# Cross-attention steps moved between attention's query blocks, with four smaller edits of a decoder layer

## What is computed

```
h = rms_norm(x);  proj = h @ w_in
A: mLSTM, chunkwise matrix memory, 4 heads of 256             -> hm (2048 x 1024)
B: latent attention, 8 heads, causal softmax, q.k over 192, v of 128
   ha = attention(q, k, v) * silu(a_z)                        -> ha (2048 x 1024)
C: cross attention into 256 memory tokens, 4 heads of 256
   hc = softmax(c_q k_mem / 16) v_mem * silu(c_z)             -> hc (2048 x 1024)
merged = sigmoid(g_m) * (hm @ w_br_m) + sigmoid(g_a) * (ha @ w_br_a) + sigmoid(g_c) * (hc @ w_br_c)
out = rms_norm(x + merged @ w_out)
```

## Time and profile before

| what | value |
|---|---|
| runs of the kernel before | 3058.36, 2812.47, 2815.47 us |
| median | 2815.47 us |
| profiled execution, device time | 2817.33 us |
| span of its slowest core (7) | 2816.1 us |
| spans of cores 0 to 6 | 2811.3, 2792.0, 2789.0, 2808.3, 2811.6, 2793.5, 2797.1 us |

### The profile page before, as it was taken

The page is one execution under the profiler, slowest core; times in us unless marked ns, Lnnn a source line. Parts: engine busy times, 40 slices in busy tenths (PEclk is TensorE's granted clock), DMA queues, the critical chain, the costliest instruction groups (busy, mean ns, idle before and its releaser), DMA issues.

```text
span 2816.1 us, 42574 instructions; the slowest of 8 cores (2789.0 to 2816.1 us)
## 1 busy us (share of the span) xinstructions
PE 2698.2 (96%) x14245; PEld 1303.7 (46%) x14245; DVE 943.8 (34%) x1783; ACT 771.4 (27%) x1551; POOL 446.6 (16%) x643
## 2 busy tenths in 40 slices
PE   7999998998998999999999989999999999999998
PEld 4445444444454444455555444444444444444443
DVE  5356673364654433232223341111113211111123
ACT  5223321112444443444444441111112111111111
POOL 2101101131232221000000000332321122122111
PEclk9999999999999999999999999999999999999999
DMA  9648553254463664446325477557558744444453
GB/s 256 172 88 180 103 108 66 41 115 98 95 113 92 146 158 123 110 101 136 93 63 116 112 200 206 109 110 147 117 116 221 212 79 79 79 69 78 68 150 120
DMA packets 198678, 340.98 MB, mean 121 GB/s; under 512 B 47617, under 2 KB 142145, under 8 KB 191809
## 3 DMA queue, kind: packets, MB, share of 16 engines
q0 software_dynamic: 31392, 138.26, 29.3%
q1 hardware_dynamic: 167074, 200.01, 24.2%
HBM read 390.19 MB, written 86.28 MB: 169 GB/s over the span
## 4 chain that ended last, share of the span: by engine, by line
PE 84%; DMA 9%; DVE 3%; issue 2%; ACT 1%; SPq 1%; POOL 0%; DVEq 0%; ACTq 0%; POOLq 0%
PE bk L505 22%; PE bk L1485 20%; PE bk L493 14%; PE bk L1493 10%; PE bk L1664 7%; PE bk L1325 2%; PE bk L1295 2%; PE bk L1297 2%; DMA m_mv<-MV 1%; DMA m_cq<-CQT 1%; DMA m_hb<-wOUT 1%; DMA m_wgb<-wGB 1%; DMA ACC<-m_tmpc 1%; DMA m_w<-wA 1%; DMA HCT<-m_hcT 1%
## 5 line engine op out<-in xcount | busy, mean ns | idle before, releaser
L505 PE MATMUL bk<-m_w,m_hT 128*128 128x512 bf16 x3072 | 728.8, 381 | 16.7 <-DMA m_w<-wA 6.0
L1485 PE MATMUL bk<-m_hT,m_wgb 128*128 128x512 bf16 x3072 | 706.4, 380 | 4.2 <-ACT m_sg L1490 2.5
L1485 PEld LDWEIGHTS bk<-m_hT,m_wgb 128*128 128x128 bf16 x3072 | 299.1, 98 | 358.1 <-issue 7.6
L505 PEld LDWEIGHTS bk<-m_w,m_hT 128*128 128x128 bf16 x3072 | 296.3, 98 | 347.1 <-issue 30.5
L1493 PE MATMUL bk<-m_hb,m_wgb 128*128 128x512 bf16 x1536 | 368.0, 380 | 3.0 <-DVE m_tmpc L1498 2.6
L493 PE MATMUL bk<-m_hT,m_w 128*128 128x512 bf16 (+1 forms) x1600 | 359.4, 380 | 7.0 <-DVE m_t L862 6.3
L1498 DVE SCALAR_TENSOR_TENSOR m_tmpc<-m_sg,bk 128x512 f32<-128x512 f32 x160 | 110.0, 688 | 654.4 <-PE bk L1485 446.5
L1490 ACT ACTIVATE m_sg<-bk 128x512 f32<-128x512 f32 x192 | 114.7, 598 | 778.0 <-PE bk L1485 728.2
L493 PEld LDWEIGHTS bk<-m_hT,m_w 128*128 128x128 bf16 (+1 forms) x1600 | 156.7, 99 | 191.3 <-issue 13.1
L1300 ACT ACTIVATE m_Pa<-bk 128x512 bf16<-128x512 f32 (+1 forms) x320 | 169.0, 533 | 236.8 <-PE bk L1297 150.9
L1493 PEld LDWEIGHTS bk<-m_hb,m_wgb 128*128 128x128 bf16 x1536 | 149.5, 98 | 179.3 <-issue 5.6
(11 more groups left out here) (182 smaller groups left out, 2239.5 us busy)
## 6 DMA issues: line engine op xcount, KB each, us to landing
m_wgb<-wGB POOLq DMA_DIRECT2D x96, 768.0 KB, 7.8
m_w<-wA POOLq DMA_DIRECT2D x72, 512.0 KB, 12.6
m_xt<-x SPq DMA_DIRECT2D x16, 1024.0 KB, 12.1
m_xo<-x SPq DMA_DIRECT2D x16, 1024.0 KB, 10.8
out<-m_xo SPq DMA_DIRECT2D x15, 1024.0 KB, 4.3
m_w<-wMEM POOLq DMA_DIRECT2D x16, 512.0 KB, 18.2
ACC<-m_tmpc SPq DMA_DIRECT2D x32, 256.0 KB, 7.2
m_accl<-ACC SPq DMA_DIRECT2D x16, 512.0 KB, 5.1
```

The lines of the kernel that those rows point to most:

```text
L505: fw.op("pe", lambda e: e.matmul(bk[:, 0:ncols], lhsT=src(kc, tt * 128, 128), rhs=w[:, kc, 0:ncols], start=(kc == 0), stop=(kc == KC - 1)) ...
L1485: fw.op("pe", lambda e: e.matmul(gb[:, 0:512], lhsT=w[:, kc, :], rhs=mg_t["h0"][:, kc, tcs], start=(kc == 0), stop=(kc == 15)), reads=[w.r ...
```

## The change

- Attention finishes a query tile (reciprocal and scaling) right after its last key tile, the diagonal one, instead of all four at the block's end.
- `cross()` becomes a generator that is stepped from inside `mla()`. The dense stream raises a flag (`cz_done`) when gate `CZ[1]` is done and its input tiles are freed. At the first block end after that, the cross loads of the first two steps are issued; at each later block end, an even share of the 16 steps runs, in place of two of the three units that a block end counted. What is left runs after attention.
- `tmpc` has four buffers instead of two until the late chunks are done.
- The eight pieces of output weights 0 and 1 are issued one per 56 TensorE instructions instead of all at once.
- In each half's output projection, the first two pairs of token tiles run quarters 0 and 1 for both, then 2 and 3 for both. Their sums of squares get four small tiles (`sts`) instead of two, and the loads of x for tiles 4 and 5 move from units 9 and 10 to 13 and 14.

```diff
--- before.py
+++ after.py
@@ -1230,3 +1230,3 @@
 
-        all_az0 = []
+        all_az0, cz_done = [], []
 
@@ -1309,2 +1309,4 @@
 
+            cr = cross()
+            begun = []
             loads(0)
@@ -1327,2 +1329,14 @@
                           reads=[P.r, vx.r], writes=[r_bo])
+                if kt == 0:
+                    has = []
+                if kt >= 4 * qb:
+                    qt = kt
+                    bo, r_bo = o_of(qt - 4 * qb)
+                    sc = nxt_st()
+                    fw.op("dve", lambda e: e.reciprocal(out=sc[:, 0:1], in_=bo[:, 128:129]), reads=[r_bo], writes=[sc.r])
+                    ha = nxt_hat()
+                    fw.op("dve", lambda e: e.scalar_tensor_tensor(out=ha[:], in0=bo[:, 0:128], scalar=sc[:, 0:1], in1=az[:, qt, :],
+                                                                  op0=ALU.mult, op1=ALU.mult),
+                          reads=[r_bo, sc.r, az.r], writes=[ha.r])
+                    has.append(ha)
                 if qb == 1 and kt == 0 and h + 1 < 8:
@@ -1337,13 +1351,2 @@
                     continue
-                has = []
-                for q4 in range(4):
-                    qt = 4 * qb + q4
-                    bo, r_bo = o_of(q4)
-                    sc = nxt_st()
-                    fw.op("dve", lambda e: e.reciprocal(out=sc[:, 0:1], in_=bo[:, 128:129]), reads=[r_bo], writes=[sc.r])
-                    ha = nxt_hat()
-                    fw.op("dve", lambda e: e.scalar_tensor_tensor(out=ha[:], in0=bo[:, 0:128], scalar=sc[:, 0:1], in1=az[:, qt, :],
-                                                                  op0=ALU.mult, op1=ALU.mult),
-                          reads=[r_bo, sc.r, az.r], writes=[ha.r])
-                    has.append(ha)
                 if qb % 2 == 0:
@@ -1363,7 +1366,24 @@
                 tails.append(tail)
-                yield 3
+                yield 1
+                if cz_done and not begun:
+                    begun.append(31 - 4 * h - qb)
+                    yield from step_of(cr)
+                    yield 1
+                elif begun:
+                    k = begun[0] - (31 - 4 * h - qb)
+                    for _ in range(16 * k // begun[0] - 16 * (k - 1) // begun[0]):
+                        yield from step_of(cr)
+                else:
+                    yield 2
             tails.pop(0)()
             yield 1
+            yield from cr
             ar.free(kr, qns, qrs, kns, vxs, azs, haTs, Ps, hat, stB)
 
+        def step_of(g):
+            for c in g:
+                if c is None:
+                    return
+                yield c
+
         def cross():
@@ -1408,3 +1428,3 @@
             ld = [loads(*steps[0]), loads(*steps[1])]
-            yield 6
+            yield None
             nxtP = scores(*steps[0], ld[0][0])
@@ -1455,3 +1476,2 @@
             yield from mla()
-            yield from cross()
 
@@ -1522,5 +1542,6 @@
             ar.free(hT[1], t32s, t16s)
+            cz_done.append(True)
             mg_t["sg2"] = ar.alloc("sg", [128, 2, 512], F32, nres=2)
             mg_t["sg"] = rotate([(mg_t["sg2"][:, k, :], mg_t["sg2"].res[k]) for k in range(2)])
-            mg_t["tmps"], mg_t["o"] = mk("tmpc", 2, [128, 512], F32)
+            mg_t["tmps"], mg_t["o"] = mk("tmpc", 4, [128, 512], F32)
             yield from first_share(range(16 - N_LATE), d2_banks)
@@ -1536,2 +1557,5 @@
         run(first_share(range(16 - N_LATE, 16), bankset(*range(8))))
+        ar.free(mg_t["tmps"][2:])
+        del mg_t["tmps"][2:]
+        mg_t["o"] = rotate(mg_t["tmps"])
         ar.free(mg_t["hb0"])
@@ -1544,3 +1568,3 @@
         xos = [ar.alloc("xo", [128, D], F32, nres=4) for _ in range(2)]
-        sts, _ = mk("stO", 2, [128, 8], F32)
+        sts, _ = mk("stO", 4, [128, 8], F32)
         g_banks = bankset(*range(8))
@@ -1552,5 +1576,5 @@
 
-        def load_wo(n4):
+        def load_wo(n4, parts=range(4)):
             v, r = wo_view[n4]
-            for q in range(4):
+            for q in parts:
                 k = slice(4 * q, 4 * q + 4)
@@ -1622,4 +1646,4 @@
                     if th == 0 and c == 6 and b == 1:
-                        load_wo(0)
-                        load_wo(1)
+                        for i in range(8):
+                            fw.later(56 * i + 1, lambda i=i: load_wo(i // 4, (i % 4,)))
                     if c == 13 and b == 1:
@@ -1641,3 +1665,3 @@
 
-            for u, t8 in ((0, 2), (0, 3), (9, 4), (10, 5), (17, 6), (18, 7)):
+            for u, t8 in ((0, 2), (0, 3), (13, 4), (14, 5), (17, 6), (18, 7)):
                 at(u, x_load, xos[t8 % 4], th * 8 + t8)
@@ -1651,3 +1675,6 @@
             units = []
-            for pr in range(4):
+            for h2 in range(2):
+                for pr in range(2):
+                    units += [(pr, n4, j, n4 == 3, False) for n4 in (2 * h2, 2 * h2 + 1) for j in range(2)]
+            for pr in (2, 3):
                 seq = (0, 1, 2, 3) if pr < 3 else (2, 3, 0, 1)
@@ -1659,3 +1686,3 @@
                 t8 = pr * 2 + j
-                xt, sc = xos[t8 % 4], sts[j]
+                xt, sc = xos[t8 % 4], sts[t8 % 4]
                 cols = slice(n4 * 512, (n4 + 1) * 512)
```

## The result

The changed kernel needs 2784.11 us (median of four runs, 2782.70 to 2787.24), the kernel before 2814.28 (median of four): ratio 0.9896, 95% interval 0.9882 to 0.9910. So it is about 1% faster, which is clear of the spread of the runs but less than the 2% that the prediction called measurable. The forecast was 2780, the range 2770 to 2799. The total came out near the forecast; several of the terms that make it up did not, as the experiments show.

What follows compares the result with a forecast made beforehand. TensorE, busy 96% of the span, was taken as the bound, the slowest core setting the time. Terms 11 + 8 + 8 + 1.5 + 7 = 35.5 us on core 7 gave a median of about 2780 us, range 2770 to 2799.

Steps and rivals of the forecast that it cites:

- nobody waits: Attention's tile finishes: the last reciprocal and scaling are covered by other matmuls and delay nothing; gain 11 us.
- the pair is done first: On VectorE in attention: reciprocal and scaling end before the next mask can start, its exponential taking 534 ns on ScalarE.
- my bound of 12.4: Most that finishing tiles singly could gain: attention's waits for reciprocal and scaling, 8.3 + 4.1 us over 31 block ends.
- SP releases them as soon as the stores ahead of them in its queue are ready: A pair's first cross loads find their buffer free and wait only for one ACC store per 10 us and a HAT store.
- So the load waits nearly go: Cross steps between attention blocks: query-load waits, 6.8 us before, nearly vanish, with 1.4 us left for late loads.
- cross loads wait in SP's queue: Rival, 0.08: cross loads stand behind attention's loads or stores as often as before, spreading cross steps gives nothing; 2788 us.
- the 10.4: TensorE's idle time in the old cross stretch of 102 us, the upper bound for spreading the steps; 8 forecast.
- the handovers: Eight places where the next block's fourth tile takes the last cross tile's bank; cost 1 us, bounds 0 and 5.2.
- one core's 8.2 us: Core 7 after the mix: 5.1 us in stops and 3.1 to the clock, removed by four buffers on slow cores; 8 taken.
- late transfers: Rival, 0.13: the fourth output weight lands late or branch loads hold stores too long; about 15 us return, 2795 us.
- Score banks: Rival, 0.04: 96 cross takings of the two shared score banks each wait for a ScalarE op; 51 us, 2831 us.
- that rival's 25 us: Rival, 0.02: the clock falls at each of eight handovers as at the stops after the mix; 25 us return, 2805 us.

Runs made afterwards that it cites:

- parts 3 to 5: Four result buffers, output weights issued piecewise and projection units reordered, on the kernel before; three-stage sum 1663.6 us, against 1667.5 before.
- with the mask first: The changed kernel with a query tile's reciprocal and scaling emitted behind the scores of the item after next; 2781.6 us.
- parts 1, 2 and 3 alone: The kernel before with only tiles finished singly, only cross steps between blocks, or only four result buffers; 2806.1, 2831.4 and 2814.2 us.
- two result buffers: The changed kernel with two `tmpc` buffers in place of four; 2789.0 us.

## Why the prediction came out right, and where it was not

Forecast were 35 us by the medians, measured 30. The terms, for core 7 as forecast, and as the mean of the cores measured in steps (parts 3 to 5, then 1, then 2):

| part | forecast | measured |
|---|---|---|
| 1 | 11 | 14.3 |
| 2 | 8 | 6.2 |
| 3, 4, 5 | 8 + 1.5 + 7, part 3 on slow cores only | 3.9 |
| sum | 35.5 | 24.4 |

That the total lies near the forecast is in part luck: the five parts were worth 24.4 us in the mean, 11 less than their sum. The slowest cores of the two profiled executions are 34.5 us apart: 24.4 of it in the stages, 3.6 in an earlier start of attention (1124.7 and 1121.0 us in the mean), in code that is the same, and the rest because the slowest core lay nearer to the others. Over ten executions of the kernel before and seven of the changed one, the slowest core is 13 us above the mean of the cores before and 9 after; no experiment explains that.

**Part 1: the gain was there, the reason "nobody waits" was not.** The step that failed is "the pair is done first". I asked whether the next mask could start before the pair and forgot the dense gate operation that may stand ahead of both; the in-order engine then delivers the mask late. It cost 6.6 us of waits on core 7. The gain came out all the same, and with the mask first the first stage alone falls by 328.1 - 313.8 = 14.3 us (the same figure as in the table by chance), over my bound of 12.4 for attention as a whole. The term that the bound lacked: a wait also breaks a run of short matmuls. A product alone takes 0.22 us, four in a row 0.39, so one in a run adds (0.39 - 0.22) / 3 = 0.06, and each wait costs up to 0.16 on top of itself. The first stage of before on core 7, its waits of this kind:

```profile
PE bk L1325 <- DVE m_stB L1343: 6.3, 21, 0.3
PE bk L1325 <- DVE m_hat L1345: 3.1, 10, 0.3
```

That is 31 waits, 9.4 us, and up to 31 x 0.16 = 5.0 that shows as busy time. In the changed kernel 10 such waits are left. The products with v alone (busy of PE and PEld, in the first stage, before and then changed, core 7):

```profile
1133.20:1461.30 328.10, 85.38 (x770) 60.38 (x770) 1.00 0.44 102
```
```profile
1126.30:1445.50 319.20, 81.10 (x770) 59.59 (x770) 1.00 0.46 106
```

The same 770 products are 4.3 us shorter; 21 waits fewer explain up to 21 x 0.16 = 3.4 of it. From before to the version with the mask first, TensorE's idle time in this stage goes from 14.9 to 6.4 us and its busy time from 313.2 to 307.6 (core 7): 8.5 + 5.7 = 14.2. The bound had only the first of the two. The Trainium skill (TensorE: Matmul & The Clock Gate, Single matmul latency) has (398 + N) / 2.4 ns for a matmul of N columns that runs alone; by it 129 columns come to an estimate of 220 ns, and the rows agree.

**Part 2: right in size, wrong in its account.** "SP releases them as soon as the stores ahead of them in its queue are ready" took no account of how late these stores are, and "So the load waits nearly go" failed: the waits stayed at 5 to 6 us in the mean, on core 7 all in the second step of a pair, for loads that are issued in the first. SP waited 113.5 of 240 us for the data of the ACC stores, and the loads stood behind these. This is the rival "cross loads wait in SP's queue", which was right about the queue and wrong in that part 2 then gives nothing. The 13.4 us that the rival went by are those of a load of 512 KB, twice the size of a query load, and show no order in a queue. The Trainium skill (DMA: Bandwidth & Descriptors, Queues, rings and completion order) has each engine consume a queue's descriptors in ring order; what held the loads here came ahead of that, SP's wait before it issues the store, and no run here shows the rule itself. The gain came from the other waits: those of the old cross stretch for what is not a load (3.6 of the 10.4), and those of attention's last blocks for exponentials and tile finishes, which were not in the sum. What I had put at 1 us for the handovers, products that wait for a cross tile's finish, came to 0.5. The waits for ScalarE fell, I take it, since ScalarE's operations for the cross steps now lie in a longer stretch (a reading, not an experiment): they run from 1467 to 1649 us on core 7, where I had said 1470 to 1600.

**Part 3: mis-sized, and by the wrong division of cores.** I took the earlier trace rows to show slow and fast cores. In nine other executions of the kernel before, beside these experiments, the slower one of two neighbouring cores changes from run to run, so one core's 8.2 us was partly a matter of that run. Nor did the stop keep to the slow cores in the execution that I read: TensorE waits for a result buffer on all but cores 2 and 6, for 1.7 to 2.7 us, cores 1 and 5, which I had counted as fast, among them. Core 1, from 1680 to 2060 us:

```profile
PE bk L1493 <- DVE m_tmpc L1498: 2.2, 1, 2.2
```

And core 6, for which only parts 1 and 2 were forecast (18 to 19 us), lost 22.3 us in the three stages, core 7 27.6 of its 35.5. The mechanism stands (two buffers bring back the stop); its size is 3.0 to 3.7 us in the mean, and nothing when part 3 is tried alone.

**Parts 4 and 5: the start of the second half was put at nothing.** The second half's projection kept its 110.5 us, as forecast, and the first projection itself came to 2157.8 - 2047.3 = 110.5 us on core 7, as forecast, without a wait for weights. But the first half's end is when the last stores start, and the load that waits for them is due right after: HCT waits rose from 1.9 to 3.5 us in the mean, 0.6 of new ones for HMT came in, and the last stage kept all but 1.3 us, where 7 were forecast. A stage that ends 7 us earlier reaches its next load 7 us earlier. This was the rival "late transfers", by another transfer than the two it named.

**Score banks and clock.** The cross scores' new waits at the score banks are 2.2 us, far from that rival's 51. The clock in the middle stage is 1.00 in the mean (0.99 before), so that rival's 25 us did not come either, though its evidence was thin: the earlier trace rows has one core, which kept clock 1.00 through a wait of 3.5 us, while cores 0, 2, 4 and 6 had 0.97 in the same 102 us, and the changed kernel shows a fall behind a wait of 2.30. What stays open: why part 1 is worth 4.4 us in the middle stage beside parts 3 to 5 and 1.8 alone (where its waits for result buffers were 2.8 us against 1.7, which explains about 1); and the 0.6 to 2.3 us by which the last stage got longer in the runs of parts 1, 2 and 3 alone, if that is more than chance.

## What to carry to other kernels

When an operation is moved earlier on an in-order engine, list everything that can stand ahead of it there, other streams' operations too, and put what the bound engine reads ahead of what only frees a buffer. A load issued from a queue that also carries stores is as late as the store in front of it: issue it one more step ahead rather than ask how fast it lands. And follow a removed wait to the next load in line, since several waits of one stretch hide each other and a part tried alone can show nothing of what it is worth in company.

## What had not been expected of the hardware

- A wait in a run of short matmuls costs more than the idle time that the profile shows: a product of 129 columns took 0.22 us by itself, while each further one of a run added 0.06.
- Neighbouring cores (0 and 1, 2 and 3, and so on) ran unequally in ten executions of the kernel before: 11 to 20 us apart, now the one slower, now the other. In seven of the changed kernel they were 2.5 to 15 apart. The Trainium skill (HBM Reference, Specifications) has two cores share the bandwidth of one memory domain; no run here shows that this is the cause.
- The clock after a stop did not go by the stop's length alone. In the kernel before, a wait of 3.45 us in the cross steps was followed by the full rate (groups of four matmuls in 1.02 and 1.03 us, below, core 7). In the changed kernel one of 2.30 was followed by one such group and then by one in 1.74 (core 7). With two result buffers, after one of 3.83 between merge tiles, eight matmuls at once took 3.57 instead of 1.89 (core 6).

```profile
1627.04 1.02 PE L1391 MATMUL bk<-m_cq,m_kmT 128*128 128x512 bf16 x4 [3.45 <-DMA m_cq<-CQT]
1627.90 1.03 PE L1493 MATMUL bk<-m_hb,m_wgb 128*128 128x512 bf16 x4
```
